# Second attention: third turned group behind the first scores, the convolution's high parts in the first two units, the output's square behind the first turned copy

## The reference, cut to what matters

```
s = einsum('bqhmd,bkhmd->bhmqk', q, k)
a = softmax(s / 8, axis=-1)
a = a[:, :, 0] - lam * a[:, :, 1]
o = einsum('bhqk,bkhe->bqhe', a, v)
attn = rmsnorm_2(o, subln_g) * 0.8
u = gc * xc
conv = gb * conv3(u)
out = concatenate([attn, conv]) @ w_out
```

## Time and profile before

| what | value |
|---|---|
| median of 3 runs | 2697.93 us |
| the profiled execution, its own time | 2696.95 us |
| span of its trace | 2695.7 us |
| TensorE (PE) busy | 2598.3 us, 96% of the span |
| VectorE (DVE) busy | 1829.8 us, 68% |
| ScalarE (ACT) busy | 1304.7 us, 48% |
| GpSimd (POOL) busy | 515.2 us, 19% |
| mean granted clock of TensorE | 0.986 |
| the 32 units' turned groups (L3133) | 1748.2 to 1958.4 us |

### The profile page before, as it was taken

How to read it: one execution, slowest core, us unless ns; L and a number is a source line. 1 busy time by engine, 2 the same in 40 slices (tenths; PEclk the granted TensorE clock), 3 DMA queues, 4 the chain that set the end, 5 groups by cost and what they waited for, 6 DMA issues and landing times. The chain is left out here.

```text
span 2695.7 us, 35795 instructions
## 1 busy us (share of the span) xinstructions
PE 2598.3 (96%) x13421; PEld 2202.4 (82%) x13421; DVE 1829.8 (68%) x2193; ACT 1304.7 (48%) x2014; POOL 515.2 (19%) x729
## 2 busy tenths in 40 slices
PE   8999999999999999999999999999997799999996
PEld 7799998888898787778888898778876688888885
DVE  4288887632458888875557333489845788888887
ACT  4255653511343333333445121288723477777775
POOL 5722220000022222221101310022233100000102
PEclk9999999999999999999999999999998899999998
DMA  8700001111323445657655422001144699999998
GB/s 299 268 25 25 24 21 40 47 47 50 123 100 107 148 151 176 198 178 287 202 194 173 110 61 67 5 21 36 67 150 192 236 386 395 395 396 394 395 394 271
DMA packets 249515, 461.90 MB, mean 171 GB/s; under 512 B 16588, under 2 KB 138176, under 8 KB 247936
## 3 DMA queue, kind: packets, MB, share of 16 engines
q1 hardware_dynamic: 218944, 352.73, 37.3%
q0 software_dynamic: 30288, 106.84, 12.1%
q10 hardware_dynamic: 112, 0.03, 0.0%
HBM read 384.79 MB, written 65.32 MB: 167 GB/s over the span
## 5 line engine op out<-in xcount | busy, mean ns | idle before, releaser
L508 PE MATMUL ps<-r,r 128*128 128x512 f32 (+4 forms) x10508 | 2302.0, 377 | 9.1 <-DVE r L672 3.8
L508 PEld LDWEIGHTS ps<-r,r 128*128 128x128 f32 (+1 forms) x10508 | 1879.7, 188 | 360.3 <-issue 9.6
L485 ACT ACTIVATE r<-f 128x2048 fp32r<-128x2048 f32 (+2 forms) x339 | 503.8, 1495 | 386.3 <-PE ps L508 383.2
L3739 DVE TENSOR_TENSOR r<-f,r 128x2048 fp32r<-128x2048 f32 x188 | 429.2, 2291 | 63.8 <-ACT r L485 62.4
L493 DVE TENSOR_TENSOR r<-f,r 128x1024 fp32r<-128x1024 f32 (+1 forms) x151 | 168.1, 1128 | 319.0 <-ACT r L485 319.0
L508 PE MATMUL ps<-f,f 128*128 128x128 f32 (+1 forms) x1218 | 153.3, 277 | 3.9 <-ACT f L1288 3.3
L508 PEld LDWEIGHTS ps<-f,f 128*128 128x128 f32 x1218 | 145.0, 193 | 6.8 <-issue 5.6
L876 DVE SCALAR_TENSOR_TENSOR f<-f,misc,f 128x1023 f32<-128x1023 f32 (+29 forms) x120 | 146.4, 1260 | 0.0
L2018 ACT ACTIVATE r<-f 128x512 fp32r<-128x512 f32 x140 | 87.1, 629 | 71.2 <-PE ps L508 57.4
L3757 POOL DMA_INDIRECT ff_scratch<-f,misc x15 | 29.0, 1934 | 474.1 <-ACT f L3868 442.4
L3269 DVE TENSOR_REDUCE misc<-ps 128x1 f32<-128x1280 f32 x64 | 95.1, 1487 | 21.6 <-PE ps L508 21.3
(11 more groups left out here) (349 smaller groups left out, 2282.8 us busy)
## 6 DMA issues: line engine op xcount, KB each, us to landing
f<-in_w_gate_dram SPq DMA_DIRECT2D x64, 1024.0 KB, 8.3
f<-in_w_up_dram SPq DMA_DIRECT2D x64, 1024.0 KB, 10.1
f<-in_w_down_dram SPq DMA_DIRECT2D x64, 1024.0 KB, 8.0
f<-in_w_in_dram SPq DMA_DIRECT2D x56, 512.0 KB, 4.4
f<-in_w_ada_dram SPq DMA_DIRECT2D x96, 256.0 KB, 4.8
f<-in_w_ffn_in_dram SPq DMA_DIRECT2D x80, 256.0 KB, 4.0
hid_scratch<-f POOLq DMA_DIRECT2D x77, 256.0 KB, 2.8
f<-hid_scratch SPq DMA_DIRECT2D x35, 512.0 KB, 5.0
```

The lines of the kernel that those rows point to most:

```text
L485: self.act.activation(hi, raw, ACT.Copy).then_inc(self.sem(st.name + "_hi"), 1)
L508: return self.pe.matmul(o, left, right, start=start, stop=stop, skip_group_check=True)
L3739: self.dve.tensor_tensor(es.lo[i % 4], es.raw[i % 8], es.hi[i % 4].bitcast(F32), ALU.subtract).then_inc(self.sem("e_lo"), 1)
```

## The change

Four things are done in the second attention.

1. In steps 2 to 31 PE issues turned groups 0 and 1, then the first column group of the scores of half 1 (two products), then turned group 2, then the other two column groups. In steps 32 and 33 the order stays.
2. The square of unit u's output (`square_o`) leaves `copy_v` and is issued one step later, behind ACT's copy of turned group 0. The last one (unit 31) is issued at the head of step 34.
3. The four high parts of the convolution are made two at the end of step 0 and two in step 1, ahead of the exponential of half 1, where one stood at the end of each of the steps 0 to 3.
4. `pe_scores2` takes the column groups to be done as an argument; its waits belong to the first part, its signal to the last.

```
@@
-    def pe_scores2(self, u, mp):
+    def pe_scores2(self, u, mp, parts=(0, 1, 2)):
...
-        if u:
+        if u and parts[0] == 0:
             pe.wait_ge(*sem(f"a2_exp{mp}", u))
...
-        for c in range(3):
+        for c in parts:
...
-        t.then_inc(sem(f"a2_qk{mp}"), 1)
+        if parts[-1] == 2:
+            t.then_inc(sem(f"a2_qk{mp}"), 1)
...
-            if 2 <= u <= n + 1:
-                turn_p(u - 2)
-            if 0 < u < n:
+            if 2 <= u < n:
+                turn_p(u - 2, (0, 1))
+                self.pe_scores2(u, 1, (0,))
+                turn_p(u - 2, (2,))
+                self.pe_scores2(u, 1, (1, 2))
+            elif n <= u <= n + 1:
+                turn_p(u - 2, (0, 1, 2))
+            if u == 1:
                 self.pe_scores2(u, 1)
...
                 act.copy(o.rearrange("p a b -> p (a b)"), ps[:, 6 + k % 2, 0:(4, 4, 2)[g] * P]).then_inc(
                     sem("a2_p"), 1)
+                if g == 0 and u >= 1:
+                    square_o(u - 1)
...
             act.activation(self.OM2[j], ps[:, 6 + k % 2, 0:P], ACT.Copy, scale=self.r8[u % 3][0]).then_inc(
                 sem("a2_val"), 1)
+
+        def square_o(u):
+            j = u % 2
             act.wait_ge(*sem("a2_val", u + 1))
...
             act.activation(self.SQ2, self.OM2[j], ACT.Square, accum_out=self.sub_ss[j]).then_inc(sem("a2_sq"), 1)
+
+        def high_conv(first, last):
+            for m in range(first, last):
+                ct = (m + 3) % 4
+                act.activation(self.MX[0][:, 4 + ct, :], self.CV[ct], ACT.Copy).then_inc(sem("mc_hi"), 1)
...
+            if u == n + 2:
+                square_o(n - 1)
...
+            if u == 1:
+                high_conv(2, 4)
             if u < n:
                 expo(u, 1)
             if 2 <= u <= n + 1:
                 copy_v(u - 2)
-            if u < 4:
-                if u == 0:
-                    act.wait_ge(*sem("c2_o", 8))
-                    act.wait_ge(*sem("cv2_mm", 24))
-                ct = (u + 3) % 4
-                act.activation(self.MX[0][:, 4 + ct, :], self.CV[ct], ACT.Copy).then_inc(sem("mc_hi"), 1)
+            if u == 0:
+                act.wait_ge(*sem("c2_o", 8))
+                act.wait_ge(*sem("cv2_mm", 24))
+                high_conv(0, 2)
```

More of the change, by code:

```diff
@@ L3107, in pe_scores2 @@
         sk = self.stacks[h % 2]
-        if u:
+        if u and parts[0] == 0:
             pe.wait_ge(*sem(f"a2_exp{mp}", u))
-        if i == 0:
+        if i == 0 and parts[0] == 0:
             pe.wait_ge(*sem("sk_hi", 6 * (h + 1)))
@@ L3124, in pe_attention2, with turn_p @@
         n = len(self.PAIRS)
-        def turn_p(u):
+        def turn_p(u, groups):
             pe.wait_ge(*sem("a2_mix", u + 1))
-            for g in range(3):
+            for g in groups:
                 k = self.turn_use("p", u, g)
```

## The result

The changed kernel takes 2764.52 us (median of 6 runs, 2762.41 to 2766.66) against 2700.78 us for the kernel before in the runs beside it (6 runs, 2696.41 to 2701.72). The ratio is 1.024, with a 95% interval of 1.0229 to 1.025: slower by some 64 us. The forecast was 2754 us, in a range from 2704 to 2776.

The account below looks back on a forecast made before the run. PE was taken to bound the attention, with the late square making its turned output wait for POOL. From 2696.95 us, +36 (collision), +21 (clock), -0.5 (start) and 0 (end) gave 2753.5, against the median 2754; range 2704 to 2776.

Parts of the forecast that it names:

- the collision: Attention steps 4 to 31: POOL's product held behind DVE's mix, steps of 7.89 us, +36.1 us.
- The chain of the square: Attention (T: start of a step's first turned piece): square T + 1.12, product T + 2.55, output T + 4.29.
- The one step before in which the mix had been first: Step 8 of the earlier profile: mix 0.64 us ahead, product 1.40 us; taken as the pattern of each step.
- The split worth nothing: Attention, before group 2: the removed wait gains nothing, as PE only comes earlier to the longer wait.
- three single waits: PE's longest waits around the attention: 1.87 and 1.78 us followed by half clock, 1.96 us not.
- PE's clock: Attention: the new idle brings half clock in 14 of 28 steps, 1.5 us each, +21 us; bounds 0 to +42.
- the 2 in 3 of the rows: Two of PE's three longest waits around the attention were followed by half clock; shaded to 14 of 28 steps.
- The start: Convolution parts, steps 0 to 3: T of step 4 unmoved within a microsecond, -0.5 us, bounds -2 to +1.
- The end: Steps 32 and 33: product and turned output move by 0.3 us or so; 0 us, bounds -1 to +1.
- The chain alone: Rival, attention: no collision, only POOL's chain late, steps of 6.90 us, +8.4, 2705 us; chance 0.12.
- The clock held: Rival, attention: the collision comes but PE's clock holds, 2733 us; chance 0.20.

Follow-up runs that it names:

- the square alone: Kernel before the change with only the square moved behind ACT's copy of group 0: 2738.30 us, ratio 1.0144.
- the mix that waits: Changed kernel with one wait more, DVE's mix waiting for POOL's product of that step: 2718.44 us, ratio 1.0075.
- the product on ACT: Two runs, changed kernel with POOL's product made by ACT behind the copy of group 2: 2704.63 us; with the square also put back, 2696.49 us.
- the unsplit version: Changed kernel with the square put back, the product on ACT and the turned groups in one piece again: 2693.85 us, ratio 0.9975.
- PE kept busy: Changed kernel with ten products of ones on PE before the turned output in steps 3 to 31: 2739.60 us, ratio 1.0146.
- the convolution's parts alone: Kernel before the change with only the convolution's four high parts moved into steps 0 and 1: 2698.93 us, ratio 0.9992.
- the product on ACT, square behind the first copy: Changed kernel, its square left late, with the product made by ACT behind the copy of group 2: 2704.63 us, ratio 1.0014.
- the square put back: Changed kernel with the square again directly behind `copy_v`, before the copy of group 0: 2703.79 us, ratio 1.0014.

## Why the prediction was right

The mechanism was right, a collision of POOL's product with DVE's mix and half clock in part of the steps. In parts of the span, the forecast was 36 us for the collision, 21 for the clock, -0.5 at the start and 0 at the end, 56.5 us together; measured were 37 and 28 (64.8 together), -2.9 and +5.8, in all 67.7. The result lies 10.5 us above the forecast, mostly by the clock's term and the end.

*The chain of the square.* It predicted a square at T + 1.12, POOL's product at T + 2.55 and the mix at T + 2.10; all three were measured to 0.01 us in twenty of the 28 steps. The one step before in which the mix had been first was a true pattern: turned output at T + 4.29 there, T + 4.28 in the changed kernel, and full-clock steps of 7.86 to 8.10 us for the 7.89 forecast. Eight of the steps stand 0.12 us later (T + 4.40), the mix with them. The term of +36.1 us is confirmed by the square alone: +38 us, with no loss of clock. That the product was held by the mix is shown from two sides, by the mix that waits and by the product on ACT.

*The split worth nothing.* Right: the wait for the copy went from 12.5 to 0.5 us in a kernel that got no faster, and, which is the test, with the product on ACT the unsplit version is as fast. What the prediction did not see is that it can do harm: some 6 us with the square in its old place, and with the late square it makes one wait out of two, and the half clock comes with it, 26 us between "the square alone" and the changed kernel. I had costed the clock by three single waits, and not asked which part of the change brings it.

*PE's clock.* The term was mis-sized. 14 steps were taken, 17 of 28 were hit; the price of one was put at 1.5 us and is 9.50 - 7.87 = 1.63 to 9.63 - 8.00 = 1.63. (The 8.00 us are 7.87 and the 0.12 us by which the mix is later in such steps.) 17 x 1.63 = 28 us, where +21 stood. The rate, 17 of 28, is near the 2 in 3 of the rows, which I had shaded down; but two of three single waits are no rate, and that it came out so close is partly luck. That it is the clock, and not something with the same rhythm, is shown by PE kept busy: no long step, 25 us less.

*The start.* T of step 4 came 2.9 us earlier, past the bound of 2 us. The values of step 2 no longer stand behind a convolution part. Part of it is the clock, which was 0.79 over the 8 us around step 2, and not 0.57 as in the earlier trace rows. And 1.5 us of it are there at T of step 2 already (1746.79 against 1748.31), which need not be the edit's: the run with the square alone has the same program up to that point, and its T of step 2 is 1750.98.

*The end.* Forecast 0, measured +5.8 us behind T of step 32. Steps 32 and 33 are as forecast (7.13 us for step 32, against 7.58). The rest lies after the attention, where the changed kernel has stretches at a lower clock and the kernel before has none. After a wait of 1.97 us for the last turned output PE takes 15.46 us for the next 60 products, where the kernel before, after one of 1.96 us, takes 13.88. The mean granted clock of this part:

```profile
2009.00:2140.00 131.00, 125.38 (x663) 105.65 (x661) 60.13 (x92) 36.94 (x70) 30.10 (x53) 0.96 0.35 133
```

```profile
1949.00:2074.00 125.00, 118.77 (x649) 100.16 (x648) 60.13 (x92) 36.83 (x70) 31.28 (x53) 1.00 0.36 134
```

(the first the changed kernel, the second the kernel before). Why waits of the same length were followed by half clock in one and not in the other is open; it was not tried. In the other runs this part differs too, by up to some 6 us; in that of the convolution's parts alone, whose program is that of the kernel before from step 4 on, it is 751.0 us against 746.2. So most of the 5.8 us need not be the edit's.

*The rivals.* The chain alone (steps of 6.90 us, 2705 us) is what the product on ACT came close to, 2704.6 us; but that the two times agree is luck, since its plain steps are shorter (6.60 us) and four longer ones, of 7.6 to 9.9 us, make up for it. The clock held (2733 us) is what the square alone gave, 2738.

## What to carry to other kernels

Before moving a small operation behind another, follow its result to the last engine that waits for it, and look at what else runs there at that moment: here 0.47 us of delay on one 0.31 us square put a 0.61 us product behind a 1.55 us operation of another engine and made each step 1.3 us longer (37 / 28). One row in which the order was the other way gave the whole price in advance. And removing a short wait in front of a long one can cost: PE's clock stayed up with idle pieces of 0.24 and 1.4 us in each step, and fell in 17 of 28 steps with one of 1.8 or 1.9.

## What was not expected of the hardware

The waits that cost the clock are hardly longer than those that did not. Waits of 1.39 to 1.53 us, one in each of 28 steps, never brought the half clock; waits of 1.80 to 1.93 us did in 17 of 28. Nearly equal waits had unequal ends: one of 1.82 us was followed by half clock and one of 1.80 us two steps later was not (the product on ACT, square behind the first copy), and so it went with one of 1.97 and one of 1.96 us at the end of the attention. What tells them apart is open.

DVE and POOL hold each other very unevenly. Where the mix is first, POOL's product ends 0.48 us after the mix, and POOL's factor is held in the same way (1.83 us instead of 0.55). Where POOL's product is first by 0.02 us, the mix loses 0.14 us. Where POOL's factor is under way (in step 13 of the changed kernel from 1844.72, with the mix from 1844.94), the mix takes its usual 1.55 us. Of the rule in the Trainium skill (SBUF — State Buffer, "SBUF: two separate sides"), an exclusive lock for the whole instruction of whoever starts first, the trace agrees with the half that POOL waits for DVE, and not with the other half. When the mix came, POOL's operation had 0.59 us left in the first of these two cases (1848.21 - 1847.62) and 0.35 us in the second.

A kernel can fall into a rhythm of its own. With the square put back, short and long steps alternate, 5.82 and 7.90 us, because a step without a collision puts the next one into it; over the attention the mean is 6.8 us (190.2 / 28), more than the 6.6 us of the kernel before (184.8 / 28).
